# Seven half-width products in place of eight in ten turns of gate and linear projections, with stored sums of weight tiles

## The reference

```python
def swiglu(h, w_gu, w_dn):
    g, u = jnp.split(h @ w_gu, 2, axis=-1)
    return (jax.nn.silu(g) * u) @ w_dn
# h: 512 x 1024, w_gu: 1024 x 5632 (gate and linear side by side), w_dn: 2816 x 1024

# second_block:
        h = rmsnorm_2(x, g_pre[l, 0]) * (1 + sc1) + sh1
        x = x + 0.5 * gt1 * rmsnorm_2(swiglu(h, w_gu1[l], w_dn1[l]), g_post[l, 0])
        ...
        h = rmsnorm_2(x, g_pre[l, 2]) * (1 + sc3) + sh3
        x = x + 0.5 * gt3 * rmsnorm_2(swiglu(h, w_gu2[l], w_dn2[l]), g_post[l, 2])
```

## Time and profile before

| | |
|---|---|
| three runs | 2290.18, 2293.87, 2295.51 us; median 2293.87 |
| profiled execution | 2295.32 us, span 2293.3 us |
| TensorE busy | 2258.4 us (98%), 10438 matmuls |
| weight loads | 1858.3 us (81%) |
| VectorE, ScalarE, GpSimd busy | 1015.3, 902.7, 1056.0 us |
| mean granted clock of TensorE | 0.987 |
| read from and written to device memory | 250.02 and 12.58 MB |

### The profile page before, as it was taken

One profiled execution on the slowest core, in us unless ns is written; L12 is line 12 of the kernel. 1 busy time (PEld: TensorE's weight loads), 2 busy tenths in 40 slices (PEclk: granted clock), 3 DMA queues, 4 the chain that ended last, 5 costly groups with the idle time before them and its releaser, 6 DMA issues.

```text
span 2293.3 us, 32856 instructions
## 1 busy us (share of the span) xinstructions
PE 2258.4 (98%) x10438; PEld 1858.3 (81%) x10438; DVE 1015.3 (44%) x1670; ACT 902.7 (39%) x1632; POOL 1056.0 (46%) x812
## 2 busy tenths in 40 slices
PE   8999999999999999999999999999999999999997
PEld 7888888888888888888888778888677787888886
DVE  6899785527623415110115235555565555100112
ACT  4334663333222333332333354444665453332332
POOL 3455555454444454444445443333322454444444
PEclk8999999999999999999999999999999999999999
DMA  4333444337747532333332323334312432333331
GB/s 150 97 97 96 145 120 158 96 107 288 269 134 230 174 97 78 93 100 97 96 96 83 84 80 111 110 110 142 97 51 60 149 95 74 96 96 97 96 97 60
DMA packets 129483, 263.95 MB, mean 115 GB/s; under 512 B 14256, under 2 KB 14384, under 8 KB 128624
## 3 DMA queue, kind: packets, MB, share of 16 engines
q1 hardware_dynamic: 119520, 236.51, 34.4%
q10 hardware_dynamic: 9872, 26.25, 3.0%
HBM read 250.02 MB, written 12.58 MB: 115 GB/s over the span
## 4 chain that ended last, share of the span: by engine, by line
PE 89%; DVE 5%; issue 3%; ACT 2%; POOL 1%; DMA 0%; ACTq 0%; DVEq 0%; POOLq 0%
PE bank L1028 25%; PE bank L1030 25%; PE bank L1029 25%; PE bank L1293 2%; PE bank L1294 2%; PE bank L1295 2%; PE bank L1383 1%; PE bank L1346 1%; PE bank L1427 1%; POOL wlo L415 1%; PE bank L1449 1%; DVE bank L1712 1%; PE bank L1368 1%; PE bank L1168 0%; PE bank L1131 0%
## 5 line engine op out<-in xcount | busy, mean ns | idle before, releaser
L415 POOL TENSOR_TENSOR wlo<-raw,whi 128x512 fp32r<-128x512 f32 x750 | 985.9, 1323 | 1135.2 <-ACT whi L517 1134.1
L1028 PE MATMUL bank<-a_hi,whi 128*128 128x512 f32 x1928 | 762.1, 395 | 6.5 <-DVE a_lo L1509 2.5
L1030 PE MATMUL bank<-a_lo,whi 128*128 128x512 f32 x1928 | 751.1, 390 | 0.0
L1029 PE MATMUL bank<-a_hi,wlo 128*128 128x512 f32 x1928 | 750.6, 389 | 0.0
L517 ACT ACTIVATE whi<-raw 128x512 fp32r<-128x512 f32 x750 | 468.0, 627 | 644.8 <-PE bank L1030 571.7
L1028 PEld LDWEIGHTS bank<-a_hi,whi 128*128 128x128 f32 x1928 | 362.0, 188 | 88.5 <-issue 7.2
L1030 PEld LDWEIGHTS bank<-a_lo,whi 128*128 128x128 f32 x1928 | 361.9, 188 | 76.3
L1029 PEld LDWEIGHTS bank<-a_hi,wlo 128*128 128x128 f32 x1928 | 362.2, 188 | 75.2 <-issue 1.4
L1028 PE MATMUL bank<-b_hi,whi 128*128 128x512 f32 x852 | 335.0, 393 | 0.5 <-DVE b_lo L1850 0.3
L1029 PE MATMUL bank<-b_hi,wlo 128*128 128x512 f32 x852 | 332.3, 390 | 0.0
L1030 PE MATMUL bank<-b_lo,whi 128*128 128x512 f32 x852 | 332.1, 390 | 0.0
(11 more groups left out here) (274 smaller groups left out, 1832.3 us busy)
## 6 DMA issues: line engine op xcount, KB each, us to landing
raw<-d_stream SPq DMA_DIRECT2D x750, 256.0 KB, 2.6
G<-d_ada SPq DMA_DIRECT2D x72, 512.0 KB, 5.2
spill_rv<-tmp ACTq DMA_DIRECT2D x32, 256.0 KB, 2.1
G<-spill_rv ACTq DMA_DIRECT2D x8, 1024.0 KB, 8.3
G<-d_x ACTq DMA_DIRECT2D x4, 512.0 KB, 5.6
spill_ga<-sq ACTq DMA_DIRECT2D x8, 256.0 KB, 3.7
G<-spill_ga ACTq DMA_DIRECT2D x1, 2048.0 KB, 8.4
G<-d_x ACTq DMA_DIRECT2D x1, 2048.0 KB, 13.7
```

The source lines that it names most:

```text
L415: pool.tensor_tensor(wlo[:, s % SRING, :], raw[:, s % RING, :], whi[:, s % SRING, :].bitcast(F32), ALU.subtract).then_inc(lo_done, 1)
L1028: pe.matmul(out_ps, w_hi, hi[:, k, :], start=first and q == 0, stop=False)
L1029: pe.matmul(out_ps, w_lo, hi[:, k, :], start=False, stop=False)
L1030: mm = pe.matmul(out_ps, w_hi, lo[:, k, :], start=False, stop=last and q == len(ks) - 1)
```

## The change

In stages "gu2b" and "gu3b", now "wg2b" and "wg3b", the product of a 2x2 group of weight tiles (two inner tiles, gate and linear) with a 2x2 group of values (two inner tiles, the two halves of the 512 tokens) is made by seven products of half width (256 columns) in place of eight (Winograd's form of Strassen's scheme). For that:
- Sums of values: four per pair of inner tiles, made once for each feed-forward part from `a_hi` + `a_lo` during the first four turns of stage a (`turn_values`, `turn_hi`, `turn_lo`) and kept split in `t_hi` and `t_lo`.
- Sums of weight tiles: the 40 given panels of stage b are loaded once more during stages "gu..a" and "dn..a" (`given_load`), VectorE makes four sums of each (`panel_sums`), ScalarE's queue stores them in device memory (`made_store`, into `spill_rv` and `spill_ga`, which are free then).
- In the stage itself each pair of output tiles takes 8 panels in place of 4: four given ones, of which 384 columns are split, and four of stored sums.
- The banks are used as two sets of four. A pair of output tiles is put together from four banks by VectorE (`products_pair`), with semaphore `w_free` when all are read. Behind the last pair TensorE waits for it before the down stage.
- All tensors are placed by hand, and `SIL` lies elsewhere.

The diff, cut to its core:

```diff
+H = T // 2
+PRODUCTS = {"wg2b": 5, "wg3b": 5}
+PLAIN_TURNS, MADE_PER_TURN = 2, 4
+GIVEN_RING, MADE_RING = 4, 3
+def columns_of(p):
+    return slice(P, SOME) if is_given(p) else slice(0, SOME)
...
@@ sync
+            def given_load(n, m):
+                t = MADE_IN_ALL * (n - 2) + m
+                if m >= GIVEN_RING:
+                    sp.wait_ge(sums_made, t - GIVEN_RING + 1)
+                sp.dma_start(GIVEN[:, m % GIVEN_RING, :].rearrange("p (a c) -> p a c", c=2 * P), halves_of(n, m // 8, m % 8))\
+                  .then_inc(given_landed[m % GIVEN_RING], 16)
+            def products_turn(n, i):
+                base = PLAN[f"wg{n}b"][0]
+                for s in range(8):
+                    p = base + 2 * s
+                    sp.wait_ge(lo_done, i * 16 + (p + 1))
+                    sp.dma_start(raw[:, p % RING, :].rearrange("p (a c) -> p a c", c=2 * P), halves_of(n, i, s))\
+                      .then_inc(raw_landed[p % RING], 16)
+                    p += 1
...
+                    sp.dma_start(raw[:, p % RING, :], sums).then_inc(raw_landed[p % RING], 16)
@@ gpsimd
-                pool.tensor_tensor(wlo[:, s % SRING, :], raw[:, s % RING, :], whi[:, s % SRING, :].bitcast(F32),
+                c = columns_of(s)
+                pool.tensor_tensor(wlo[:, s % SRING, c], raw[:, s % RING, c], whi[:, s % SRING, c].bitcast(F32),
@@ scalar
+            def made_store(n, m):
+                t = MADE_IN_ALL * (n - 2) + m
+                act.wait_ge(sums_made, t + 1)
+                to = spill_rv[:, m, :] if m < 32 else spill_ga[:, m - 32, :]
+                act.dma_start(to, MADE[m % MADE_RING]).then_inc(made_out[m % MADE_RING], 16)
...
+                def first_product(i, w):
+                    wait_used(act, name, i, 8 * w + 7)
+                    act.wait_ge(w_free, i * 2 + (g0 + w + 2))
+                    act.activation(WFIRST, bank[4 * (w % 2)][:, 0:H], ACT.Copy).then_inc(w_first, 1)
+                def silu(i, w):
+                    act.wait_ge(w_free, i * 2 + (g0 + w + 3))
+                    act.activation(WG, WG, ACT.Silu, scale=-1.0).then_inc(w_silu, 1)
...
+                def pair(i, w, before=True):
+                    s = 8 * w
+                    if before:
+                        first_product(i, w - 1)
+                    tick(name, i, s, 3)
+                    if before:
+                        silu(i, w - 1)
+                    tick(name, i, s + 3, 1)
+                    if before:
+                        hi(i, w - 1)
+                    tick(name, i, s + 4, 4)
@@ tensor
+            def products(ps, w_slot, c, hi, lo, first, last):
+                w_hi, w_lo = whi[:, w_slot, c * P:(c + 1) * P], wlo[:, w_slot, c * P:(c + 1) * P]
+                pe.matmul(ps, w_hi, hi, start=first, stop=False, skip_group_check=True)
+                pe.matmul(ps, w_lo, hi, start=False, stop=False, skip_group_check=True)
+                return pe.matmul(ps, w_hi, lo, start=False, stop=last, skip_group_check=True)
...
+                    products(bank[at][:, lower], p % SRING, 2, a_hi[:, k0, lower], a_lo[:, k0, lower], first, last)
+                    products(bank[at + 1][:, lower], p % SRING, 3, a_hi[:, k1, lower], a_lo[:, k1, lower], first, last)
+                    products(bank[at + 2][:, upper], p % SRING, 1, t_hi[:, q, 3, :], t_lo[:, q, 3, :], first, last)\
+                        .then_inc(used, 1)
+                    p += 1
+                    pe.wait_ge(lo_done, i * 16 + (p + 1 + RING))
+                    products(bank[at + 3][:, lower], p % SRING, 0, t_hi[:, q, 0, :], t_lo[:, q, 0, :], first, last)
+                    products(bank[at + 3][:, upper], p % SRING, 1, t_hi[:, q, 1, :], t_lo[:, q, 1, :], False, last)
+                    products(bank[at + 1][:, upper], p % SRING, 2, t_hi[:, q, 2, :], t_lo[:, q, 2, :], False, last)
+                    products(bank[at + 2][:, lower], p % SRING, 3, a_hi[:, k1, upper], a_lo[:, k1, upper], False, last)\
+                        .then_inc(used, 1)
...
+                        pe.wait_ge(w_free, PAIRS_AT[name] + 2 * PRODUCTS[name] + 1)
+                    for m in range(KD):
+                        tile_packed(down, m, K, OPB, opb, FILL_B[f"ffn{n}{half}"])
@@ vector
+                own.next(dve.tensor_tensor(halves(u), halves(bank[at + 1][:, :]), twice(WFIRST), ALU.add))
+                own.next(dve.tensor_tensor(halves(WSUM), halves(bank[at + 3][:, :]), twice(v), ALU.add))
+                own.next(dve.tensor_tensor(g, bank[at + 2][:, :], WSUM, ALU.add))
+                dve.tensor_tensor(last, bank[at + 3][:, 0:H], WSUM[:, H:T], ALU.add).then_inc(w_free, 1)
+                dve.wait_ge(w_silu, i * 2 + (g0 + w + 1))
+                dve.tensor_tensor(tmp[:, w % 2, :], WU, WG, ALU.mult).then_inc(w_prod, 1)
+                dve.wait_ge(b_hi_w, i * 2 + (fill + skip + w + 1))
...
+                for i in range(1, FA // 2):
+                    for x in range(MADE_PER_TURN if i >= PLAIN_TURNS else 0):
+                        panel_sums(n, (i - PLAIN_TURNS) * MADE_PER_TURN + x)
+                    if i < 4:
+                        turn_values(fill, b, i)
+                    gate_pair(a, i, 0, at)
```

More of the change, by code:

```diff
@@ L12 @@
+import math
 from contextlib import ExitStack
@@ L45 @@
 SOME = 4 * P
+H = T // 2
+PRODUCTS = {"wg2b": 5, "wg3b": 5}
+PLAIN_TURNS, MADE_PER_TURN = 2, 4
+GIVEN_RING, MADE_RING = 4, 3
+PAIRS_AT = {}
+_w = 0
+for _n, _t in PRODUCTS.items():
+    PAIRS_AT[_n] = _w
+    _w += 2 * _t
 def k_panels(K, tiles):
@@ L398, in _ @@
             ada_run("gu1b", 6, 3)
-            load_run(b + 24, NPANELS - b - 24)
+            at = b + 24
+            for n in (2, 3):
+                first = PLAN[f"gu{n}a"][0] + 8 * PLAIN_TURNS
+                load_run(at, first - at, -sums_before(at))
+                for p in range(first, PLAN[f"wg{n}b"][0]):
+                    load(p, 0, 0, -sums_before(p))
+                    to = made_beside(n, p)
+                    if to is not None:
+                        given_load(n, to)
+                products_run(n)
+                at = PLAN[f"dn{n}b"][0]
+            load_run(at, NUNITS - at, -sums_before(at))
             for k in (0, 1, 2, 6, 3, 4, 7, 5):
@@ new lines, in made_turn @@
+            def made_turn(n, i):
+                name, b, m0 = f"gu{n}a", n - 2, (i - PLAIN_TURNS) * MADE_PER_TURN
+                if i == 1:
+                    turn_hi(b, 0)
+                for x in range(5):
+                    tick(name, i, x, 1)
+                    if i >= PLAIN_TURNS and x:
+                        made_store(n, m0 + x - 1)
+                if i < 4:
+                    turn_hi(b, i)
+                gate_hi(name, i, 0, 5)
+                tick(name, i, 6, 1)
+                gate_hi(name, i, 1, 7)
@@ new lines, in seven_products @@
+            def seven_products(n, norm, fill):
+                for half, K in (("a", FA), ("b", FB)):
+                    down = f"dn{n}{half}"
+                    if half == "a":
+                        wide_stage(f"gu{n}a", OPA, opa, fill, FA // 2, late=n == 3)
+                    else:
+                        name = f"wg{n}b"
+                        with pe.Fori(0, PRODUCTS[name]) as i:
+                            products_pair(name, i, 0, down)
+                            products_pair(name, i, 1, down)
+                        pe.wait_ge(w_free, PAIRS_AT[name] + 2 * PRODUCTS[name] + 1)
+                    for m in range(KD):
+                        tile_packed(down, m, K, OPB, opb, FILL_B[f"ffn{n}{half}"])
+                if n == 2:
+                    sums_between(0, norm)
+                else:
+                    sum_up(norm)
@@ L1654, in _ @@
             dve.wait_ge(vchain, 1)
-            for s, n in ((lo_done, RING), (used, SRING), (ada_used, ADA_SLOTS)):
+            for s, n in ((lo_done, RING), (used, SRING), (ada_used, ADA_SLOTS), (w_free, 2)):
                 dve.memset(small[:, 4, 0:1], 0.0).then_inc(s, n)
```

269 lines of the change are left out of this document (241 added, 28 removed).

## The result

The changed kernel took **2272.61 us** (median of 4 runs, 2272.31 to 2276.02), the kernel before 2293.44 (4 runs, 2290.18 to 2295.51). The ratio is 0.9914, 95% interval 0.9897 to 0.9931: faster by 20.8 us by the medians.

The account below looks back on a forecast made before the run. TensorE, busy 98% of the span, was taken as the bound. Products -15.9, end-of-stage pauses +6.6, clock +1.7 and loop waits +2.0 sum to -5.6 us, forecasting 2289 us, range 2279 to 2306.

Parts of the forecast that it names:

- The end of the stage: Before each second down projection, TensorE stands still 3.3 us until the last pair is combined: +6.6 us for two stages.
- A down projection that starts without pause: Listed sign in the profile, at the start of the down stages, that the forecast was wrong; 3.3 us idle was expected.
- The clock term: After the pause before a down projection, 3.4 us at half clock, counted for one of two stages: +1.7 us.
- Loop ends and waits: In the rewritten stages, more frequent computed waits cost TensorE 0.1 us a pair: +2.0 us, ends 0 and 6.
- The products: In the rewritten stages, 84 matmuls of 256 columns at 0.120 us, 10.09 us a pair instead of 10.88: -15.9 us.
- GpSimd: Makes the low parts in the rewritten stages: 10.04 us a pair, level with TensorE's 10.09; no cost counted, ends 9.1 and 11.24.
- The first halves: Added loads, sums, stores and conversions in the first halves and first down projections stay hidden: no cost.
- rival 1: Rewritten stages: nothing lost per matmul, starts 0.112 us apart; 2288 us, or 2275 to 2276 with GpSimd fast; chance 0.27.
- rivals 1 and 3: The second of these: doubled weight loads cost array time in the rewritten stages, starts 0.136 us apart; 2315 us, chance 0.12.
- against 2: Case that GpSimd becomes the slower bound in the rewritten stages, up to 11.24 us a pair; 2311 us, chance 0.10.
- against 4: Case that stored sums arrive late in the rewritten stages, 1 us per 8 panels, 20 times; about 2308 us, chance 0.06.

Follow-up runs that it names:

- halves: Kernel before, each 512-column matmul of the two second-half stages issued as two of 256 columns, same weights loaded anew; 2303.62 us beside 2291.67 for the kernel before.
- full_low_part: Changed kernel, with the given panels split and their low part made over all 512 columns instead of 384; 2292.75 us, ratio 1.0003 to the kernel before.
- sums_only: Kernel before with the added loads, sums, stores and value conversions, sums never read back, eight products of 512 columns kept; 2292.41 us, ratio 1.0002.
- after_again: The changed kernel run once more, unaltered, against the kernel before; 2271.76 us, ratio 0.9916.
- last_operand_later: Changed kernel, with six matmuls of output tile 1 moved ahead of those needing the late operand in the down stages; 2271.17 us, ratio 0.9913.
- shorter_at_same_place: Kernel before, 35 matmuls of 512 columns left out of each of the two stages, output incomplete, no sums; 2273.73 us, ratio 0.9923.

## Why the prediction was wrong, point by point

**The end of the stage: the step that failed.** The prediction said that "the first matmul of the down projection waits until the last pair is combined (w_free)" and put +6.6 us on it. The semaphore starts at 2 (two free sets of banks) and the target is 11, so the wait is met when 9 of the 10 pairs are combined. That was at 1176.06, 6.7 us before the first down matmul (the ninth pair's last addition starts at 1175.64 and takes 0.42). The wait guards the set of banks that the down stage uses, and the tenth pair used the other one. wait_last_pair, which raises the target by one, gives the priced pause (3.11 us idle, twice, and the stages 3.3 longer). In place of +6.6 the step is +1.8, and that comes from another wait, the one for the last operand, which I had set to nothing because I took the pause to cover it. Working: the operand is complete 6.1 us after the stage's end, tile 0 asks for it after 24 matmuls, 5.4 us. Against the forecast this is -4.8 us. "A down projection that starts without pause" was the prediction's own sign of being wrong, and it is what the trace shows.

**The clock term (+1.7) hung on the same pause.** It fell away with it: the rows of both down stages have the full clock.

**Loop ends and waits (+2.0).** Nothing: TensorE is busy 99.7 of 99.7 us. Against the forecast -2.0.

**The products (-15.9).** Mechanism right, size a little low. 840 starts in 99.73 us are 0.1187 each, a pair 9.97 us against the 10.09 worked out: -18.2 for the 20 pairs. Against the forecast -2.3. In halves the starts are 0.120 apart whatever the two operands; in the first stage of the changed kernel the means by operand run from 0.117 (from `t_hi,whi` to `t_hi,wlo`) to 0.120 (from `a_lo,whi` on). Why some are shorter is open.

**GpSimd.** Named rightly as what has to keep up, sized 10.04, measured 9.51. The single operations of the pair at 1119.70 take 1.28 to 1.30 us at 512 columns and 1.02 to 1.03 at 384 where nothing stands beside them, as counted, but each starts some 0.05 us before the one ahead of it has ended, and of the two collisions one is nearly gone. The one with VectorE's product is there: the product is stretched to 1.4 us and GpSimd's operation beside it takes 1.48. VectorE's low part starts at 1129.27, when GpSimd had ended (at 1129.21) and was waiting for ScalarE until 1129.70, so only its end meets the next operation:

```profile
1126.89 1.44 DVE L1950 TENSOR_TENSOR tmp<-G 128x512 f32<-128x512 f32 x1 [0.70 <-ACT G L779]
1129.27 0.69 DVE L1953 TENSOR_TENSOR b_lo<-tmp,b_hi 128x512 f32 x1 [0.93 <-ACT b_hi L783]
```

In full_low_part going from 384 to 512 columns costs 7.8 us in each stage (107.5 against 99.7).

**The first halves.** The forecast was no cost, and sums_only measured none (interval -0.07% to +0.1%).

With the measured figures the sum is -18.2 + 1.8 = -16.4 against -5.6: of the 10.8 between them, 6.5 are pause and clock, 2.3 the products, 2.0 the loop ends.

**What is left: about 4 us.** Measured are -20.8 and -20.2 (after_again), with intervals from -15.8 to -23.6 and from -16.3 to -22.2, so 16.4 is just inside both and the rest is barely shown. The profiled executions say where such amounts lie. In the kernel before, the stretch from the first down stage to the next rewritten one, and the stretch at 1317.7 in it:

```profile
1317.70:1324.40 6.70, 6.70 (x15) 4.78 (x15) 0.00 (x0) 0.17 (x1) 0.41 (x1) 0.50 0.14 39
...
1192.50:2112.60 920.10, 907.75 (x4386) 734.00 (x4386) 398.11 (x793) 410.80 (x825) 385.31 (x295) 0.99 0.32 96
```

and in the changed kernel the same work:

```profile
1182.70:2098.50 915.80, 902.72 (x4386) 730.12 (x4385) 493.35 (x941) 414.03 (x831) 394.54 (x296) 0.99 0.39 120
...
1307.00:1313.80 6.80, 6.80 (x28) 4.86 (x27) 0.00 (x0) 1.79 (x4) 2.55 (x2) 1.00 0.19 66
```

4.3 us less, though it holds the 0.9 of the late operand. At 1317.7 the kernel before runs 6.7 us at the 1.2 GHz level (15 matmuls; 28 in the changed kernel's 6.8 us at full clock), and so do shorter or longer stretches at other places. But this length differs as much between executions in which the work doesn't differ: 918.0 against 915.8 for the changed kernel itself, and 920.1 in before against 916.4 in sums_only, which is not faster by its median (the execution profiled for before was one of its slower ones, 2295.32 us, and that of sums_only the fastest of 11, 2287.79).

One profile of each kernel can't settle it, but each execution also has a mean granted clock. It is 0.9876 on average over the 55 executions of the kernels near 2292 us (before, sums_only, full_low_part) and 0.9893 over the 19 of those near 2272 (the changed kernel twice, last_operand_later, shorter_at_same_place). Among executions of one kernel 0.001 less went with some 1.2 us more (one slope fitted to all kernels with several runs). As an estimate from these figures the 0.0017 are worth 2 us, about half of the remainder. shorter_at_same_place, with 0.9898 and some 2 us more gained than its stages explain, has no seven products. So part of the 4 us goes with a kernel that is shorter at these places, and not with the products; the rest is within the noise. Why the shorter kernels were granted a little more clock, no run shows.

**The chances.** The nearest case in the text was the lower end of rival 1, 2275 to 2276, by a cause that didn't hold (starts 0.112 us apart, measured 0.1187), so that its nearness is luck. No rival came true: 0.120 held (against rivals 1 and 3), GpSimd kept up (against 2), nothing came late (against 4). The range missed because all the rivals shared the +10.3 of pause, clock and loop ends, of which 8.3 hung on the count of one semaphore; no rival doubted it.

## What to carry to other kernels

- Before a wait is priced, read the value that the semaphore starts with and ask which event meets the target. This one starts at 2 for its two sets of banks, so the target 11 is met by the ninth pair and not the tenth; here that was 11 us of difference, shown by one kernel with the target raised by one. And if a wait is struck out, the wait behind it that it had covered has to be priced.
- Before matmuls are made narrower, measure the start distance at the new width. In these stages, where each matmul loads weights of its own, it was the columns plus 0.013 us at 512 and 256 columns, and 0.112 us at 128. So seven products on half the columns paid (0.1187 against half of 0.2267, 0.113, is 5% lost for 12.5% saved); at 128 columns a start would be only 0.008 us shorter for half the work.
- Where a helper engine ends level with TensorE, measure its margin by making its work a step longer. Here 0.5 us of 10 was all there was.

## What the runs showed of the hardware

- The loss per matmul is 0.0134 us at 512 columns and 0.0133 at 256, and at 128 columns starts stand 0.1116 us apart whatever the columns need. At the lower clock level 512 columns start 0.43 us apart, in wait_last_pair as in the earlier trace rows.
- A pause of TensorE of 3.1 to 3.4 us was followed by the 0.50 clock both times in wait_last_pair, from 0.7 us after the restart the first time and already 0.7 us before it the second; the pauses of 0.94 us between two starts in the changed kernel were followed by the full clock.
- GpSimd's operation at 384 columns took 1.12 us on average beside 1.34 at 512, both with their collisions, in the whole of the changed kernel's trace (groups by shape). Single operations without a collision took 1.02 to 1.03 and 1.28 to 1.30:

```profile
L556 POOL TENSOR_TENSOR wlo<-raw,whi 128x512 fp32r<-128x512 f32 x750 | 997.8, 1338 | 1011.0 <-ACT whi L660 1009.0
L556 POOL TENSOR_TENSOR wlo<-raw,whi 128x384 fp32r<-128x384 f32 x80 | 89.7, 1121 | 6.1 <-ACT whi L660 6.1
```
